# One program for all cores becomes two: 1076 tokens without a pre-pass on even cores, 972 with it on odd ones

## What is computed

```python
ada = silu(c) @ w_ada + b_ada                       # six vectors per sequence
h = rmsnorm(x, g_pre1) * (1 + scale1) + shift1
u_pool, u_lru, g_pool, g_lru = split(h @ w_in)      # 1024 | 2048 | 2048 | 2048
y_pool = (trailing means over 2/4/8/16 tokens - u_pool) @ w_grp * scale
xc = causal conv of width 4 over u_lru
r, i = sigmoid(xc @ w_rg + b_rg), sigmoid(xc @ w_ig + b_ig)   # 8 blocks of 256
a = exp(-8 r softplus(-lam));  h_t = a_t h_{t-1} + sqrt(1 - a_t^2) i_t xc_t
merged = sigmoid(g_pool) * (y_pool @ w_pool_up) + sigmoid(g_lru) * (h @ w_lru_up)
x = x + gate1 * rmsnorm(merged @ w_out, g_post1)
h = rmsnorm(x, g_pre2) * (1 + scale2) + shift2
gt, val = split(causal conv of width 3 over h @ w_ffn_up)     # 2 x 6144
x = x + gate2 * rmsnorm((gelu(gt) * val) @ w_ffn_down, g_post2)
```

## Time and profile before

| | us |
|---|---|
| median of 3 runs (lowest, highest) | 2445.33 (2443.14, 2446.41) |
| the profiled execution | 2444.1 |
| span of its slowest core, core 1 | 2442.5 |
| span of its fastest core, core 7 | 2427.1 |
| TensorE busy in that span | 2204.9 (90%) |
| VectorE busy | 1067.0 (44%) |
| ScalarE busy | 915.6 (37%) |

### The profile page before, as it was taken

How to read it: one execution, slowest core, us unless ns; L and a number is a source line. 1 busy time by engine, 2 the same in 40 slices (tenths; PEclk the granted TensorE clock), 3 DMA queues, 4 the chain that set the end, 5 groups by cost and what they waited for, 6 DMA issues and landing times.

```text
span 2442.5 us, 42128 instructions; the slowest of 8 cores (2427.1 to 2442.5 us)
## 1 busy us (share of the span) xinstructions
PE 2204.9 (90%) x16896; PEld 1126.3 (46%) x16896; DVE 1067.0 (44%) x2195; ACT 915.6 (37%) x1232; POOL 146.5 (6%) x281
## 2 busy tenths in 40 slices
PE   2447988988899999999899999999999989999995
PEld 0122444444455555555445555555555545555552
DVE  0355897997411111110346656540006756563003
ACT  2446877885300000002364454431014434442101
POOL 0000000000000000000000000000000000000000
PEclk9568999999999999999999999999999999999997
DMA  9994666565355665569989977779778987778972
GB/s 222 251 172 75 99 109 100 96 107 100 78 96 96 112 113 95 97 108 171 201 163 195 185 137 133 136 140 183 130 130 153 197 155 134 138 138 159 198 147 95
DMA packets 61967, 338.42 MB, mean 139 GB/s; under 512 B 7504, under 2 KB 8016, under 8 KB 28240
## 3 DMA queue, kind: packets, MB, share of 16 engines
q0 software_dynamic: 39888, 273.17, 65.4%
q1 hardware_dynamic: 21888, 62.56, 8.2%
HBM read 586.69 MB, written 22.17 MB: 249 GB/s over the span
## 4 chain that ended last, share of the span: by engine, by line
PE 75%; ACT 8%; DVE 7%; DMA 6%; issue 3%; another core or an unknown queue 0%; DVEq 0%; SPq 0%; ACTq 0%; POOLq 0%
PE ps_all L260 75%; ACT sb_R L237 6%; DVE sb_R L243 3%; DVE sb_R L240 3%; DMA sb_R<-xp 2%; DMA sb_w<-w_ada 2%; DMA sb_R<-x1s 2%; ACT L237 1%; DMA sb_w<-w_in 0%; DVE sb_stl L243 0%; DVE sb_R L254 0%; DVE sb_R L263 0%; ACT sb_stl L237 0%; ACT sb_rstd L237 0%
## 5 line engine op out<-in xcount | busy, mean ns | idle before, releaser
L260 PE MATMUL ps_all<-sb_R,sb_w 128*128 128x512 bf16 (+4 forms) x14592 | 2033.0, 301 | 23.9 <-ACT sb_R L237 21.5
L260 PEld LDWEIGHTS ps_all<-sb_R,sb_w 128*128 128x128 bf16 x14592 | 1028.2, 98 | 1008.3 <-issue 50.5
L237 ACT ACTIVATE sb_R<-ps_all 128x128 f32<-128x128 f32 (+6 forms) x416 | 213.2, 545 | 666.0 <-PE ps_all L260 509.3
L243 DVE SCALAR_TENSOR_TENSOR sb_R<-sb_R,sb_cvec 128x450 f32<-128x450 f32 (+3 forms) x576 | 379.4, 706 | 26.9 <-ACT sb_R L237 15.3
L240 DVE TENSOR_TENSOR sb_R<-sb_R 128x577 bf16<-128x577 f32 (+9 forms) x148 | 166.1, 1122 | 176.3 <-ACT sb_R L237 145.0
L237 ACT ACTIVATE sb_R<-sb_R 128x578 f32<-128x578 f32 (+9 forms) x216 | 207.1, 980 | 78.8 <-DMA sb_R<-xp 43.9
L237 ACT ACTIVATE sb_wsm<-ps_all 128x577 bf16<-128x577 f32 (+1 forms) x64 | 41.9, 655 | 426.9 <-PE ps_all L260 426.4
L237 ACT ACTIVATE sb_R<-ps_all,sb_cvec 128x577 f32<-128x577 f32 (+4 forms) x184 | 170.0, 925 | 22.5 <-DVE sb_R L240 15.5
L240 DVE TENSOR_TENSOR sb_R<-sb_R,sb_mod 128x128 f32<-128x128 f32 x96 | 27.9, 291 | 292.5 <-ACT sb_R L237 289.1
L240 DVE TENSOR_TENSOR sb_R<-sb_R,sb_rstd 128x577 f32<-128x577 f32 (+5 forms) x128 | 120.1, 963 | 9.4 <-ACT sb_rstd L237 9.4
L260 PE MATMUL ps_all<-sb_R,sb_wsm 128*128 128x512 bf16 x320 | 79.3, 392 | 47.0 <-ACT sb_R L237 32.3
(11 more groups left out here) (56 smaller groups left out, 732.6 us busy)
## 6 DMA issues: line engine op xcount, KB each, us to landing
sb_w<-w_ffn_up POOLq DMA_DIRECT2D x96, 1024.0 KB, 10.8
sb_w<-w_ada POOLq DMA_DIRECT2D x48, 1024.0 KB, 16.0
sb_w<-w_ffn_down POOLq DMA_DIRECT2D x48, 1024.0 KB, 9.6
sb_w<-w_in POOLq DMA_DIRECT2D x36, 1024.0 KB, 10.4
sb_w<-w_out POOLq DMA_DIRECT2D x16, 1024.0 KB, 12.1
sb_R<-xm SPq DMA_DIRECT2D x4, 2312.0 KB, 90.4
sb_R<-xp SPq DMA_DIRECT2D x4, 2048.0 KB, 43.1
sb_w<-w_lru_up POOLq DMA_DIRECT2D x8, 1024.0 KB, 13.4
```

Source lines behind the costliest of these rows:

```text
L237: return self.P.op("act", lambda e: e.activation(out=out, in_=in_, func=func, **kw), after)
L243: return self.P.op("dve", lambda e: e.scalar_tensor_tensor(out=out, in0=in0, scalar=scalar, in1=in1, op0=op0, op1=op1), after)
L260: return self.P.op("pe", lambda e: e.matmul(out, lhsT=lhsT, rhs=rhs, start=start, stop=stop), after, signal)
```

## The change

The half of a sequence is no longer 1024 tokens, and the two kinds of core get two programs in one binary, chosen at run time by the core's number.

- Even cores (ROLE 0): the first 1076 tokens and the 128 sample tokens, N = 1204, no halo. No pre-pass: no xp, no P units, no h15 and no history matmuls. Column groups (512, 512, 180) and, in the two halves of 602, (512, 90). Eight M units, each with two ada items (ADA_N), whose tiles have fixed weight slots. `front` has an order of its own.
- Odd cores (ROLE 1): 3 + 972 + 128 columns, N = 1103; the pre-pass covers NP = 1073 tokens. Column groups (512, 512, 79) in the main pass, (512, 512, 49) in the pre-pass, (512, 40) and (512, 39) in the halves of 552 and 551. `front` keeps its order.
- Both: the factor sel and what it multiplied are gone. The pre-pass uses the ring of two triples of banks that the main units use, instead of three pairs. In `front` the sums of squares lie in banks 3 to 5, the two ada items of a pair in banks 6 and 7 instead of both in 7, and z0 computes only the first 128 features of the block; the second 128 are a job of their own in S1A(0). w_grp is loaded after the units into the place of the small gate weights. x1 is read back through two buffers instead of four. Buffers are placed anew, by formulas of the role.

```diff
-HALO = 3
-OWN = 1024
+T0 = 1076
+OWNS = (T0, SEQ - T0)
+NMAX = T0 + NSAMP
+NP = T0 - 3
...
+def set_role(role):
+    HALO = 3 * role
+    OWN = OWNS[role]
+    NPR = HALO + OWN
+    N = NPR + NSAMP
+    NA = (N + 1) // 2
+    NB = N - NA
...
+            progs = []
+            for role in (0, 1):
+                set_role(role)
+                self.P = Prog(eng_sem)
...
+                self.front()
+                self.lru()
+                self.pool_rest()
+                self.merge()
+                self.ffn()
+                progs.append(self.P)
+            def run(name):
+                def body(e):
+                    pid = e.partition_id()
+                    with e.If((pid & 1) == 0):
+                        progs[0].replay(name, e)
+                    with e.Else():
+                        progs[1].replay(name, e)
+                return body
...
         def ada_pair(i):
-            self.ada_item(1, i, 7)
+            self.ada_item(1, i, 6)
             fin[i] = self.ada_item(0, i, 7)
...
         def z0(i):
             for k in (2 * i, 2 * i + 1):
-                for c in range(2):
-                    for gi, (c0, c1) in enumerate(gP):
-                        t = self.MM(self.ap_ps(z0b[c], c1 - c0, c0), w[:, k, c * 128:(c + 1) * 128], hp[:, k, c0:c1],
...
+                for gi, (c0, c1) in enumerate(groups_of(n)):
+                    self.t_z0 = self.MM(self.ap_ps(0, c1 - c0, c0), w[:, k, 0:128], h[:, k, c0:c1], k == 0,
+                                        k == DK - 1, d, k == DK - 1 and gi == 2)
...
+        ADA_N = 1 if ROLE else 2
-        ring2 = Ring([4, 0, 2])
-        ring3 = Ring([0, 3])
-        units = [("P", b) for b in range(8)] + [("M", b) for b in range(8)]
+        ring = Ring([0, 3])
+        units = ([("P", b) for b in range(8)] if ROLE else []) + [("M", b) for b in range(8)]
...
+            for c in range(2):
+                b = ring.next()
+                if i == 0 and c == 0:
+                    jobs.append((b, self.t_z0))
+                    continue
+                tok = self.job(b, nb, groups, [(wsl[:, k, c * 128:(c + 1) * 128],
...
-        x1s = [self.f32(O_X1ST + i * 4 * SB_, SB_) for i in range(3)] + [self.f32(O_X1SU, SB_)]
+        x1s = [self.f32(O_X1ST + i * 4 * SB_, SB_) for i in range(2)]
...
-        for k in range(4):
+        for k in range(2):
             fetchA(k, None)
-                     lambda k, done: fetchA(k + 4, done) if k + 4 < DK else None)
+                     lambda k, done: fetchA(k + 2, done) if k + 2 < DK else None)
```

More of the change, by code:

```diff
@@ new lines, in run @@
+            def run(name):
[6 more added lines that the diff above has]
+                return body
+            with nc.Block() as block:
+                block.tensor(run("pe"))
+                block.scalar(run("act"))
+                block.vector(run("dve"))
+                block.gpsimd(run("pool"))
+                block.sync(run("sp"))
@@ new lines, in front @@
+        M_ = ("m", xm, N, t_xm)
+        if ROLE:
+            P_ = ("p", xp, NP, t_xp)
+            squares(0, *P_)
+            ada_pair(0)
+            squares(1, *P_)
+            squares(2, *P_)
+            ada_pair(1)
+            squares(3, *P_)
+            tr = self.rsqrt(self.rstd[:, 0:NP], 3, 3, NP, [last["p"], self.t_sl])
+            normed(range(DK), xp, NP, tr, t_np)
+            h_prev(0)
+            h_prev(1)
+            squares(0, *M_)
+            ada_pair(2)
+            z0(0)
+            z0(1)
+            h_prev(2)
+            squares(1, *M_)
+            squares(2, *M_)
+            ada_pair(3)
+            z0(2)
+            h_prev(3)
+            squares(3, *M_)
+            tr = self.rsqrt(self.rstd[:, 0:N], 3, 3, N, [last["m"], t_np[DK - 1]])
+            ada_pair(4)
+            z0(3)
+            h_prev(4)
+            normed(range(0, 6), xm, N, tr, t_nm)
+            ada_pair(5)
+            z0(4)
+            h_prev(5)
+            h_main(0)
+            h_main(1)
+            normed(range(6, 11), xm, N, tr, t_nm)
+            ada_pair(6)
+            z0(5)
+            h_prev(6)
+            h_main(2)
+            h_main(3)
+            normed(range(11, DK), xm, N, tr, t_nm)
+            ada_pair(7)
+            z0(6)
+            h_prev(7)
+            z0(7)
+        else:
+            squares(0, *M_)
+            ada_pair(0)
+            squares(1, *M_)
+            squares(2, *M_)
+            ada_pair(1)
+            squares(3, *M_)
+            tr = self.rsqrt(self.rstd[:, 0:N], 3, 3, N, [last["m"], self.t_sl])
+            normed(range(0, 6), xm, N, tr, t_nm)
+            h_main(0)
+            ada_pair(2)
+            z0(0)
+            normed(range(6, 11), xm, N, tr, t_nm)
+            h_main(1)
+            h_main(2)
+            ada_pair(3)
+            z0(1)
+            z0(2)
+            normed(range(11, DK), xm, N, tr, t_nm)
+            h_main(3)
+            for i in range(4, 8):
+                ada_pair(i)
+                z0(i - 1)
+                h_main(i)
+            z0(7)
@@ L631, in S1A @@
             s = i % 2
             d = info[i]
-            if i + 1 < 16:
-                w_next.append(self.wload(self.w_in, 4 + units[i + 1][1]))
+            if i + 1 < NU:
+                w_next.append(self.wload(self.w_in, 4 + units[i + 1][1], fixed=w_slot(i + 1)))
             if i > 1:
-                self.ada_ask()
+                for a in range(ADA_N):
+                    self.ada_ask(a, None if ROLE else 1 + a)
+            if ROLE == 0 and i == NU - 1:
+                self.w_next = 3
@@ L637, in S1A @@
             wg, wgt, wgi = self.wsm_load(blk)
[L638 to L650 removed]
+            wsl, wt, wi = w_next.pop(0)
@@ L677, in S1B @@
             ph, blk = units[i]
-            n, npr, groups, nb, ring = shape(i)
+            n, npr, groups, nb = shape(i)
             s = i % 2
@@ L1146, in h_part @@
                 h2t[k] = ts
-                if H["halo"] and k == DK - 1:
-                    hh = h2[:, :, 0:HALO]
-                    t = self.Vts(hh, hh, self.sel[:, 0:1], None, ALU.mult, after=ts)
-                    for c in range(DK):
-                        h2t[c].append(t)
             for k in range(DK):
```

467 lines of the change are left out of this document (208 added, 259 removed).

## The result

The changed kernel takes 2376.3 us (2375.0 to 2376.4) against 2444.2 for the kernel before on the same chip: a ratio of 0.972 (95% interval 0.970 to 0.974), or -68 us where -37 was forecast and the range gave -12 to -58 from there. The sign was right, the size was not. Executions that something else disturbed are left out of all comparisons; a_tz has one left, and of its others only the cores of the die that was not disturbed are read (odd ones 2386.2 to 2399.4 us). In the names of the experiments a_ stands for an edit of the kernel after, b_ for one of the kernel before, and f_ for improvements on the kernel after.

What follows compares the result with a forecast made beforehand. From the merge on, matmul count times spacing bounds the kernel; before it, only partly. Odd-core terms -22 -3 -23 -8 +11 +5 +1 +5 -1 = -35 took 2444.1 to 2409, less 2 for four cores: 2407 us, range 2386 to 2432.

Steps and rivals of the forecast that it cites:

- Term 5: front up to the first gates: z0's second block moved behind it and a later xp end, +5 us (-5 to +10).
- term 4: pre-pass units: period from 20.7 to 22.4 us, +14, passage to main units giving back 3; +11 us (+5 to +20).
- Term 6: start of the two programs: odd cores jump over the even program, +1 us (0 to 7).
- Term 7: x1 fetches in ffn_up B: two buffers cover less landing time than four, +5 us (-7 to +20).
- Terms 2 and 3: narrower third column group: pool -3 and merge -20 us; main RG-LRU units about 1.0 us shorter each, -8 us.
- term 3: main RG-LRU units: the 23.8 us period falls by about 1.0 us, -8 us for eight.
- Term 1: FFN and output projection: pairs of 512 + 40 columns cost 241 instead of 245.7 ns; -22 us, projection -2.4.
- Rivals A and C: FFN's small matmul: no cheaper below 65 columns, 2432 us, 10%; or no floor, 40 columns at 19 ns, 2378 us, 3%.
- D: narrower column groups gain nothing anywhere, by the profile page's rule; 2463 us, 1%.
- rival E: even cores end last because something there goes wrong by over 100 us; 2%.
- F: the change does not act as told, front or branch costing over 35 us; 1%.

Runs made afterwards that it cites:

- a_tz: kernel after with the small h_main halo multiplication put back on VectorE of odd cores as a factor of 1.0; cores 1 and 3 took 2393.9 and 2393.6 us.
- b_notz: kernel before without VectorE's small multiplication of h_main's three halo columns by sel; ratio to before 0.985 (0.977 to 0.992).
- a_swap: kernel after with the two programs in the other order, so even cores jump and odd ones fall through; 2363.4, 2366.5 and 2373.4 us, ratio 0.970.
- experiment 8: kernel after with xp padded by a column in DRAM so its four loads are contiguous; 2372.4 to 2374.9 us, ratio to before 0.971.
- b_triples: kernel before with the pre-pass on two triples of banks instead of three pairs; ratio to before 1.001 (0.996 to 1.006).
- b_x1two: kernel before with two buffers for the x1 read-back instead of four; ratio to before 1.001 (0.996 to 1.005).
- a_allodd: kernel after with all eight cores on the odd program, even cores' outputs wrong; 2391.6 to 2399.0 us, ratio to before 0.979.
- a_late: kernel after with all cores on the odd program and even cores starting some 120 us late; odd cores took 2349.4 to 2360.2 us.
- a_wgrp: kernel after with the w_grp load issued behind the first pool group's jobs instead of in front of the queued w_in loads; 2376.1 us.

## Why the prediction was wrong

Point by point, by its own terms:

- **Term 5, front, failed in its first step, and term 4 with it.** It says that the small multiplications by sel are "gone from VectorE" and gives them no price of their own. Their busy time is nothing; their place is 19 to 23 us (b_notz, a_tz). The row that shows it stood in the trace: VectorE idle for 8.04 us before a 128x3 instruction. The earlier trace rows even had TensorE waiting 4.99 us for VectorE at 202.73, and I took that wait as given room for z0's second block instead of asking what VectorE was late for. By stages: -12 to -13 in the front, -10 in the pre-pass.
- **The rest of the front.** It measured +2.0: -12.5 for tz (a_tz), +10 for the jump (a_swap), and so +4.5 is left for all the rest. That term 5 took +5 for z0's second block and xp is no confirmation: the 4.5 is a remainder, and the term's step "those landings stay put" was not checked for xm, whose third quarter is read 21 us later than before (experiment 8). What xm, z0 and the even cores' other timetable each add is open.
- **Term 6, the jump, was mis-sized:** +1 with bounds 0 and 7, measured 8.5 at the first load and 8 to 12 at the first gates. The reasoning that failed is "the front then waits for DMA anyway": it waits for a queue that the jump starts later. Here "Runtime: NRT & Kernel Launch", section Instruction fetch mechanics, of the Trainium skill was right in kind: it lets a taken branch stall for a fetch, and the trace agrees in that whichever cores jump start late (11.79 against 3.26 us), though it does not show what they wait for; that "it would leave the sum within its bounds" was mine and false.
- **Term 4, the pre-pass.** The period was right: four inner units took 81.7 us before and 89.5 after (22.4 a unit, as forecast; 22.15 on core 3), though the ring had the smaller part in it (0.45 us a unit in b_triples, not 0.9). The passage gave back 9.3 - 0.8 = 8.5 instead of 3: 3.4 for the rings, as forecast, and about 5 that the sum did not contain; by the rows of u_lru jobs this is because main jobs and pre-pass jobs became equally long, which is read and not isolated. With tz that is the stage's 17.5 us.
- **Term 7, x1, had the wrong sign.** I took the stall of core 1 as a cost of this kernel's buffers, and added to it. The buffers are neutral (b_x1two). In the changed kernel TensorE stops when eight cores reach ffn_up B together and does not when half of them are elsewhere (a_allodd against after, a_late against a_allodd). That core 1's stall in the kernel before is of the same kind follows from this and was not tried on that kernel, where five of the eight cores, in step with the others, did not stall at all. Of the 14.4 us of the miss, 9.4 are the stall that went and 5 the cost that never came. That the even cores' new timetable would act on the odd ones is in no term and no rival.
- **Terms 2 and 3 came out smaller.** The spacing in the merge is as computed: in 50 us of it (710 to 760) 104 tiles run where 99 did, with 64 small matmuls beside them in both, 464 ns a tile instead of 487. Some 7 us were taken back, 4.4 of them by w_grp in front of w_in (a_wgrp); the rest looks like ScalarE's backlog under it. I had left w_grp out of the parts, though it was moved past a queue. The main units came 23.7 us apart at first, and 22.7 later, where 22.8 was forecast for all (the chain, for the earlier trace rows). In term 3 the parts given for TensorE (15.6, 0.8 and 8.1) come to 24.5, one of the longer units, and not to the mean of 23.8; the sum used the mean.

```profile
439.50 18.68 PE ps_all L264 x108
...
463.22 18.68 PE ps_all L264 x108
...
489.45 15.13 PE ps_all L264 x96
...
512.14 15.13 PE ps_all L264 x96
```

- **Term 1 was right in kind and a little small:** 416.5 pairs in 100 us where 415 was forecast, 5.5 ns a pair instead of 4.7. The floor is there, at 26 ns for 40 columns. Rivals A and C (407 and 424 pairs) are refuted, and so is D, since narrower third groups did make the merge's tiles shorter.
- **Even cores** were forecast at 2303 and took 2293 to 2296, 80 us ahead of the odd ones: rival E is refuted, and so is F.

That the miss is no larger is in part luck: the jump and the pool stage cost 18 us more than forecast and hid as much of what was gained.

Of the 33 us of the miss on core 1: 22.5 from tz (12.5 in the front by a_tz, 10 in the first two units), 14.4 from x1, 5.5 from the passage, 5.4 from finer spacing in FFN and output projection; against it 9 for the jump and 8.6 in pool, merge and main units. These are readings of different runs; they come to 30, and some 3 us are left to the small steps of front and pre-pass. Open are why two buffers do not shorten ffn_up B though the backlog is gone, what makes one wait for x1 stop TensorE and another not, how much of a_late's gain is due to which core, what the strided xm costs, and the rest of the passage's excess.

## What to carry to other kernels

A tiny instruction costs what the engine's queue behind it waits: before calling one "gone from the engine", look at the idle time in front of it and at what stands behind it. Where several cores run one program in step, a stall on memory can belong to the timetable of all of them; here, giving half of them other work, or another start, removed it without a change to a line of the code around it. The program that runs on the slowest cores should be the one that needs no jump. And where a change of sizes leaves a load with rows shorter than their pitch, look at how long its issue holds the engine, and move the whole row if you can.

## What was unexpected of the hardware

- Odd cores that run the same program took 2349 to 2360 us with the even ones 120 us late, 2381 to 2391 with all in step; most of it in the front, where the late cores ask for nothing (first gates at 177 to 192 against 204 to 212).
- Jumping over the other program holds the first weight load back by 8.5 us (11.79 against 3.26), and SyncE's first by 3.4 (6.17 against 2.74).
- The issue of four loads of 2146 KB kept SyncE for 22 us (34 on core 3) where rows of 1073 elements go to a pitch of 1074, and for 2.5 where both are 1074. The other loads fit: xm took 57.5 us with 1103 of 1204 to a pitch of 1104, but 4.5 before with 1156 in both and 2.0 on even cores with 1204 in both; xp took 3.5 before with 1024 in both.
- Two matmuls over the same 552 columns take 240.1 ns as 512 + 40, 235.8 as 276 + 276 and 234.2 as 472 + 80: a matmul of 40 columns costs 26 ns, which columns/2.4 plus 2.5 gives for some 56 (an estimate from these rows).
